# Splitting the even time steps of the filter spectra once more, by n mod 4, in a diffusion step on one Trainium2 core

## The reference, cut to what matters

```python
hdn = jnp.sin(f[0] * (z @ w1 + b1))
hdn = jnp.sin(f[1] * (hdn @ w2 + b2))
filt = (hdn @ w3).reshape(L, HYENA_ORDER, 2, B_WIDTH)
return filt * jnp.exp(-t * deltas)[:, None, None, :]
...
k = jnp.concatenate([h_fwd, jnp.zeros_like(h_fwd[:1]), jnp.flip(h_bwd[1:], axis=0)], axis=0)
y = jnp.fft.irfft(jnp.fft.rfft(u, n=2 * L, axis=1) * jnp.fft.rfft(k, axis=0)[None], n=2 * L, axis=1)[:, :L]
```

## Time and profile before

| | |
|---|---|
| time, median of 3 runs | 4553.84 us (4553.35 to 4554.28) |
| profiled execution, its time | 4552.56 us |
| its span, first to last instruction | 4550.8 us |
| mean granted TensorE clock | 0.968 |
| busy, share of the span | TensorE 94%, VectorE 28%, ScalarE 15%, GpSimd 5% |
| first tap matmul to last spectrum matmul | about 31.5 to 213.2 us |
| first load of the next stage | 222.53 us |

### The profile page before, as it was taken

The page is one execution under the profiler, slowest core; times in us unless marked ns, Lnnn a source line. Parts: engine busy times, 40 slices in busy tenths (PEclk is TensorE's granted clock), DMA queues, the critical chain, the costliest instruction groups (busy, mean ns, idle before and its releaser), DMA issues. The chain is left out here.

```text
span 4550.8 us, 61875 instructions
## 1 busy us (share of the span) xinstructions
PE 4266.9 (94%) x27077; PEld 3711.6 (82%) x27077; DVE 1258.5 (28%) x3031; ACT 678.8 (15%) x1683; POOL 239.3 (5%) x132
## 2 busy tenths in 40 slices
PE   8899988989987999999999999999978999999995
PEld 4667775577447999999998888888548999999995
DVE  5324453254372000000001453432481000000003
ACT  0022221100131101111101411111231110110111
POOL 0000000000220000000000300000220000000001
PEclk8999999999988999999999999999988999999998
DMA  7320001031325878788786301000425777777775
GB/s 278 112 84 26 26 3 30 28 138 58 105 100 185 304 290 309 287 302 298 292 293 233 114 28 44 26 24 15 153 93 204 279 271 282 276 272 280 280 276 204
DMA packets 147415, 785.41 MB, mean 173 GB/s; under 512 B 14792, under 2 KB 51304, under 8 KB 101258
## 3 DMA queue, kind: packets, MB, share of 16 engines
q1 hardware_dynamic: 137930, 747.89, 44.1%
q0 software_dynamic: 9216, 33.56, 3.5%
HBM read 725.20 MB, written 56.20 MB: 172 GB/s over the span
## 5 line engine op out<-in xcount | busy, mean ns | idle before, releaser
L1731 PE MATMUL PS<-arena 128*128 128x144 f32 x11264 | 1441.9, 287 | 8.0 <-ACT arena L1766 6.5
L1731 PEld LDWEIGHTS PS<-arena 128*128 128x128 f32 x11264 | 1406.8, 190 | 9.4 <-ACT arena L1766 7.3
L1716 PE MATMUL PS<-arena 128*128 128x144 f32 x5632 | 743.4, 286 | 0.0
L1716 PEld LDWEIGHTS PS<-arena 128*128 128x128 f32 x5632 | 711.3, 190 | 4.5 <-issue 4.5
L1824 DVE TENSOR_TENSOR arena<-PS,arena 128x144 f32<-128x144 f32 x352 | 108.4, 308 | 2006.7 <-ACT arena L1792 2006.7
L1792 ACT ACTIVATE arena<-PS 128x144 f32<-128x144 f32 x352 | 102.5, 291 | 1717.3 <-PE PS L1731 1717.3
L2204 PE MATMUL PS<-arena 128*128 128x256 f32 x1152 | 262.1, 387 | 11.0 <-DVEq L2531 11.0
L1367 PE MATMUL PS<-arena 128*128 128x512 f32 x576 | 259.4, 605 | 5.5 <-PEq L2574 5.0
L2204 PEld LDWEIGHTS PS<-arena 128*128 128x128 f32 x1152 | 221.5, 195 | 42.2 <-issue 12.1
L2156 PE MATMUL PS<-arena 128*128 128x256 f32 x1152 | 252.6, 380 | 1.7 <-ACT arena L2372 1.7
L2156 PEld LDWEIGHTS PS<-arena 128*128 128x128 f32 x1152 | 217.9, 191 | 31.7 <-issue 2.8
(11 more groups left out here) (328 smaller groups left out, 3378.0 us busy)
## 6 DMA issues: line engine op xcount, KB each, us to landing
arena<-expert_panels SPq DMA_DIRECT2D x352, 1536.0 KB
arena<-ada_w SPq DMA_DIRECT2D x6, 4096.0 KB, 14.3
arena<-ada_w SPq DMA_DIRECT2D x12, 2048.0 KB
arena<-odd_w_in SPq DMA_DIRECT2D x16, 1024.0 KB, 5.6
arena<-hgrn_w SPq DMA_DIRECT2D x20, 512.0 KB, 4.0
arena<-filter_spectra SPq DMA_DIRECT2D x36, 256.0 KB, 2.7
mid_rows<-arena SPq DMA_DIRECT2D x18, 512.0 KB, 2.9
filter_spectra<-arena SPq DMA_DIRECT2D x16, 512.0 KB, 2.7
```

Source lines behind the costliest of these rows:

```text
L1716: m = pe.matmul(PS[:, m_ // 3, m_ % 3 * SLOTS:m_ % 3 * SLOTS + SLOTS], s.w2[n % RING][:, m_ * P:(m_ + 1) * P], s.hid[:, f, :], start=f == ...
L1731: m = pe.matmul(PS[:, 6 + n % 2, q * 256:q * 256 + SLOTS], s.w13[n % RING][:, q, k, :], s.xs[e % 2][:, k, :], start=k == 0, stop=k == KD - 1)
```

## The change

The table of cosines and sines and the decay are put in another order of time steps (`by_four`): tap tiles 0 and 1 hold n mod 4 = 0, tiles 2 and 3 hold n mod 4 = 2, and 4 to 7 the odd ones as before. The tap matmuls of tiles 0 to 3 read every fourth column of `hdn` accordingly. The four steps of a round become two pairs. The first step of pair p takes the even time steps only, for frequency tile p: tiles 0 and 1 against bank 0 of the pair, tiles 2 and 3 against bank 1, 8 matmuls in all. ScalarE copies the first bank, and VectorE writes the difference (the even part of frequency tile p + 2) and the sum (the even part of tile p) to two buffers. The second step takes the odd time steps, for frequency tiles p and p + 2, 16 matmuls; VectorE reads both banks and makes sum and difference with the kept even parts, four operations, and ScalarE has nothing to do in it. Both 512 KB stores of a pair follow the second step.

```diff
@@ -61,6 +61,11 @@
         assert self.n - start == per, (self.n - start, per)
         self.base = 0
         self.n = start + count * per
+
+
+def by_four(m):
+
+    return np.concatenate([m[0::4], m[2::4], m[1::2]])
 
 
 def shape_constants():
@@ -96,9 +101,9 @@
             c["fold_fwd"] = both.reshape(2, nt, P, nt // 2, P).transpose(4, 1, 0, 3, 2).astype(np.float32)
             half = np.arange(L // 2).astype(np.float64)[None, :]
             w = np.pi * n.T * (4 * half + 1) / (2 * L)
-            w = np.concatenate([w[0::2], w[1::2]]).reshape(nt, P, nt // 2, P)
+            w = by_four(w).reshape(nt, P, nt // 2, P)
             c["spec_lat"] = (np.stack([np.cos(w), np.sin(w)]) / (2 * L)).transpose(3, 2, 0, 1, 4).astype(np.float32)
-            c["decay_lat"] = np.concatenate([dec[0::2], dec[1::2]]).reshape(nt, P, 512).transpose(1, 0, 2)
+            c["decay_lat"] = by_four(dec).reshape(nt, P, 512).transpose(1, 0, 2)
         bands = 16
         aa = np.float32(2.0 * math.pi / L) * np.arange(L, dtype=np.float32)[:, None] \
             * np.linspace(1e-4, bands - 1, bands, dtype=np.float32)[None, :]
@@ -376,6 +381,7 @@
                 s.prod = [at(x + b * 512, 2, 256) for b in range(2)]
                 s.prodc = at(x, 2, 512)
                 s.even = [at(y + b * 512, 512) for b in range(2)]
+                s.even2 = [at(z + b * 512, 512) for b in range(2)]
                 s.w1, s.w2 = at(take(64), 64, parts=33), at(take(64), 64, parts=64)
                 s.v4, s.c4 = at(take(64), 64, parts=4), at(take(4), 4, parts=64)
                 s.drow = at(take(1024), 2, 512, parts=1)
@@ -415,7 +421,9 @@
                         n += 2 if r == 0 and kt == 0 else (2 if r == 0 else 1)
                         sp.wait_ge(s.se, n)
                         i = 4 * r + kt
-                        sp.dma_start(specD[r, kt::4][0:2].rearrange("b p c n -> p b (c n)"), s.hst[i % 2]).then_inc(s.st[i % 2], 16)
+                        for t in range(2 if kt % 2 else 0):
+                            sp.dma_start(specD[r, kt // 2 + 2 * t::4][0:2].rearrange("b p c n -> p b (c n)"),
+                                         s.hst[t]).then_inc(s.st[t], 16)
                         if r == 0 and kt in (1, 3):
                             for half in range(2):
                                 sp.dma_start(specD[2 * (kt // 2) + half, 8],
@@ -431,8 +439,8 @@
                 n, o, cs = 8 * r + j, r // 2, slice(r % 2 * 256, r % 2 * 256 + 256)
                 if n >= 2:
                     pe.wait_ge(s.te, n - 1)
-                start = j % 4 * 256 + j // 4
-                pe.matmul(PS[:, n % 2, :], s.hdn[:, start:start + 255:2], s.w3[:, o, :, cs],
+                start, step = (j % 2 * 512 + j // 2 * 2, 4) if j < 4 else (j % 4 * 256 + 1, 2)
+                pe.matmul(PS[:, n % 2, :], s.hdn[:, start:start + 127 * step + 1:step], s.w3[:, o, :, cs],
                           start=True, stop=True).then_inc(s.tf, 1)
 
             def pe(s, pe):
@@ -478,16 +486,20 @@
                                 s.pe_taps(pe, r + 1, j)
                         if kt == 0:
                             pe.wait_ge(s.te, 8 * (r + 1))
+                        pair, odd = divmod(kt, 2)
                         if r == 0:
-                            pe.wait_ge(s.spl[kt], 16)
+                            pe.wait_ge(s.spl[pair], 16)
+                            if odd:
+                                pe.wait_ge(s.spl[pair + 2], 16)
                         b = 2 + n % 2 * 2
                         if n >= 2:
                             pe.wait_ge(s.se, n - 1)
-                        for par in range(2):
+                        for q in range(2):
+                            tile, j0, w = (pair + 2 * q, 4, 4) if odd else (pair, 2 * q, 2)
                             for d in range(2):
-                                for j in range(4):
-                                    mm = pe.matmul(PS[:, b + par, d * 256:d * 256 + 256], s.spec[:, kt, d, 4 * par + j, :],
-                                                   tap[:, d, 4 * par + j, :], start=j == 0, stop=j == 3)
+                                for j in range(w):
+                                    mm = pe.matmul(PS[:, b + q, d * 256:d * 256 + 256], s.spec[:, tile, d, j0 + j, :],
+                                                   tap[:, d, j0 + j, :], start=j == 0, stop=j == w - 1)
                         mm.then_inc(s.sf, 1)
                         n += 1
                         if 4 * r + kt in (1, 3, 5, 7, 9):
@@ -502,19 +514,17 @@
                 for layer in range(2):
                     act.wait_ge(s.a1, layer + 1)
                     act.activation(s.hdn, s.arg, ACT.Sin).then_inc(s.hok, 1)
-                n = 0
-                for r in range(4):
-                    for kt in range(4):
-                        if r == 0:
-                            n += 1
-                        i = 4 * r + kt
-                        act.wait_ge(s.sf, n + 1)
-                        if i >= 2:
-                            act.wait_ge(s.se, n - 1)
-                        if i == 0:
-                            act.wait_ge(s.hok, 3)
-                        act.copy(s.even[i % 2], PS[:, 2 + n % 2 * 2, :]).then_inc(s.ev, 1)
-                        n += 1
+                act.wait_ge(s.hok, 3)
+                for q in range(8):
+                    n = s.step(q // 2, q % 2 * 2)
+                    act.wait_ge(s.sf, n + 1)
+                    if q >= 2:
+                        act.wait_ge(s.se, s.step((q - 2) // 2, q % 2 * 2 + 1) + 1)
+                    act.copy(s.even[q % 2], PS[:, 2 + n % 2 * 2, :]).then_inc(s.ev, 1)
+
+            def step(s, r, kt):
+
+                return 4 * r + 4 + kt if r else 2 * kt + 1
 
             def dve_taps(s, dve, ch, r, j):
                 n, o, cs = 8 * r + j, r // 2, slice(r % 2 * 256, r % 2 * 256 + 256)
@@ -577,14 +587,22 @@
                         if r + 1 < 4:
                             for j in (2 * kt, 2 * kt + 1):
                                 s.dve_taps(dve, ch, r + 1, j)
-                        i = 4 * r + kt
+                        i, q = 4 * r + kt, 2 * r + kt // 2
+                        even = (s.even[q % 2], s.even2[q % 2])
                         dve.wait_ge(s.sf, n + 1)
-                        dve.wait_ge(s.ev, i + 1)
-                        if i >= 2:
-                            dve.wait_ge(s.st[i % 2], 16 * (i // 2))
-                        odd = PS[:, 3 + n % 2 * 2, :]
-                        dve.tensor_tensor(s.hst[i % 2][:, 0, :], s.even[i % 2], odd, ALU.add)
-                        ch.link(dve.tensor_tensor(s.hst[i % 2][:, 1, :], s.even[i % 2], odd, ALU.subtract))
+                        if kt % 2 == 0:
+                            dve.wait_ge(s.ev, q + 1)
+                            second = PS[:, 3 + n % 2 * 2, :]
+                            ch.link(dve.tensor_tensor(even[1], even[0], second, ALU.subtract))
+                            ch.link(dve.tensor_tensor(even[0], even[0], second, ALU.add))
+                        else:
+                            for t in range(2):
+                                if q:
+                                    dve.wait_ge(s.st[t], 16 * q)
+                                odd = PS[:, 2 + t + n % 2 * 2, :]
+                                dve.tensor_tensor(s.hst[t][:, 0, :], even[t], odd, ALU.add)
+                                m_ = dve.tensor_tensor(s.hst[t][:, 1, :], even[t], odd, ALU.subtract)
+                            ch.link(m_)
                         dve.engine_nop().then_inc(s.se, 1)
                         n += 1
                         if i in (1, 3, 5, 7, 9):
```

## The result

The changed kernel takes 4528.3 us (median of 6 runs, 4524.45 to 4533.75), the kernel before 4554.06 us (median of 6, 4552.94 to 4556.77). The ratio is 0.9947, 95% interval 0.9936 to 0.9958: 25.8 us less. The forecast was 4528.4. Both kernels were timed twice more later (experiment 9): over all three sets, 16 executions of the changed kernel and 23 of the kernel before, the means differ by 26.0 us (one more of the kernel before, at 10662 us, was a slow one and counts in none of these numbers).

The account below looks back on a forecast made before the run. The prediction took TensorE's matmuls to bound the filter stage: 27.6 us removed, less 0.5 for VectorE and 1.7 for stores at the end, gives 25.4 us gained and 4528.4 us. The range was 4525.2 to 4533.9 us.

Parts of the forecast that it names:

- What bounds the stage: Filter stage, about 46 to 222 us: TensorE's matmuls set the pace; ScalarE and VectorE stand idle waiting for them.
- 27.6 us of matmuls: Spectrum steps: 64 of 256 matmuls go, 8 half steps of 3.45 us, 27.6 us off TensorE.
- The first step priced like the others: First spectrum step, partly at the lower clock: its removed half lies behind the clock's rise, so also 3.45 us.
- Waits of TensorE at nothing: Spectrum PSUM banks: VectorE's added 10 us stay covered, tightest margins 0.6 to 0.7 us, so waits cost 0.
- Stores paired, never awaited: Spectrum stores leave as 8 pairs, closest 10.4 us apart, landing in 2.7 to 4.9 us and not queued behind loads.
- VectorE at the end, +0.5 us: Behind the last spectrum matmul: VectorE's four operations take 2.5 us where copy and operations took 1.96, +0.5 us.
- The last pair of stores, +1.7 us: End of the filter stage: two 512 KB stores leave together and share the DMA engines, landing 1.7 us later.
- Strided weights at nothing: Even tap matmuls reading every fourth column: weight loads cost 0 extra; upper side 1.2 us for six pairs of taps.
- The sum: 27.6 - 0.5 - 1.7 = 25.4 us gained in the filter stage, giving 4528.4 us, 0.56% less; chance 90%.
- VectorE gets late: Rival: VectorE's operations hold the spectrum banks; at worst 15.4 us gained, 4538.4 us; chance 5%.
- Slower by strided loads: Rival: even taps' weight loads outgrow their 0.43 us cover; over 9.1 us slower from 0.97 us a load; chance 2%.
- A hidden gain: Rival: a transfer sets the filter stage's end and hides the gain, 4553 us; chance 1%.

Follow-up runs that it names:

- experiment 9: Changed kernel with neighbouring tap columns, earlier first store and a half-bank signal: 4525.65 us against the changed kernel's 4526.35; timed again, 4524.59 against 4526.08.
- experiment 5: Changed kernel with the 8 matmuls of each first step issued twice: next stage's first load at 224.6 us, 27.4 behind the changed kernel.
- Experiment 6: Changed kernel with VectorE's four operations of each second step issued twice: next stage's first load at 205.3 us.
- experiment 7: Changed kernel with 4 matmuls in place of 8 in each first step: next stage's first load at 187.3 us.
- Experiment 8: Changed kernel with a separate signal so each first store leaves after two of four VectorE operations: next stage's first load at 196.4 us.
- experiments 2 to 4: Kernel before with only the new time-step order: 4558.65 us; changed kernel with neighbouring tap columns: first load 195.6 us; with every eighth column: 198.1 us.
- the repaired kernel: Changed kernel with neighbouring tap columns, earlier first store and a half-bank signal: 4525.65 us, timed again 4524.59 us.

## Why the prediction was right, point by point

- **What bounds the stage.** Right. Putting the 64 matmuls back brought 27.4 us back (experiment 5).
- **27.6 us of matmuls.** Right. A fell by 146.25 - 122.53 = 23.72 us. Seven half steps of 3.455 are 24.18, less 0.46 for four pairs of slow tap loads: 23.72.
- **The first step priced like the others.** It gained 3.55 us by the starts of the second step (66.94 and 63.39), 0.3 more than 3.45 less a pair of taps and 0.1 of a later start. The clock's rise 0.6 us earlier is worth that, and it moves from trace to trace.
- **Waits of TensorE at nothing.** Right, with the margins as reckoned (0.58 us where 0.6 was said). Experiment 6 used the margins up and TensorE waited where the prediction had put the last round's tightest place, by 1.94 us each time. The prediction went through the banks of the spectrum only; in experiment 7 TensorE waits for those of the taps and of the context spectrum as well.
- **Stores paired, never awaited.** Right; no wait of VectorE for a store shows.
- **VectorE at the end, +0.5 us.** 188.60 - 185.92 = 2.68 us against 215.35 - 213.19 = 2.16: +0.52.
- **The last pair of stores, +1.7 us.** The rest of B: 7.00 - 5.04 - 0.52 = 1.44. Experiment 8 shows that 1.33 of them come from two stores leaving together. The forecast was 0.26 too dear; its size had been worked out from loads of 4 MB.
- **Strided weights at nothing.** This step failed, and by a small sum only. The argument was that a step of two costs nothing and so four would not either. A load went from 0.19 to 0.305 us, 1.6 times. It stays under the 0.43 us of stream, and its excess shows at the head of each of the five pairs of even taps at the full clock: 0.11 x 5 = 0.6 us. The upper side had the mechanism, with six pairs and 1.2 us. The rival's count was wrong as well: there are 16 even taps and 32 such loads, not 32 and 64.
- **The sum.** 25.4 predicted for the stage, 25.3 in the pair of traces: the missed 0.6 us was made up by cheaper stores (0.26) and the earlier clock (0.3). Without what the clock gave it is 23.72 in A, 3.34 ahead of it (3.45 less one pair of taps) and 1.96 lost in B, 25.1 us. Against the one trace of the kernel before, the changed kernel's four give 24.7 to 26.3. The medians of the first set differ by 25.8. That the median came out within 0.1 us of the forecast is luck, since single runs of the changed kernel spread over 9 us.
- **The rivals.** *VectorE gets late* did not happen, but experiment 7 shows that it is the next thing to happen. *Slower by strided loads* would have needed 34.5 / 32 + 0.43 = 1.5 us a load (the prediction said 0.97, with twice the loads); even a step of eight takes 0.31. *A hidden gain* fell with experiment 5.

## What to carry to other kernels

Before matmuls are cut in a stage, reckon when the engine behind TensorE gives each bank back, place by place: here 0.6 us of margin made the whole gain real, and with four matmuls less in each first step TensorE runs into it. Then look at what the cut leaves behind the last matmul, because there every operation and every store counts in full; signals for half of a result put half of it back under the matmuls. Judge such a change by stretches of the trace that repeat to 0.02 us, when the whole time scatters by more than the terms in question.

## What the runs showed of the hardware

- A float32 weight load of 128 columns takes, at the full granted clock, 187 ns from neighbouring columns, 193 from every second, 305 from every fourth and 310 from every eighth (experiments 2 to 4). At the clock of 0.50 it takes about 0.33 us at each of these steps. Under tap matmuls with 0.43 us between loads the difference shows only behind a switch of work, 0.11 us each time.
- In four traces of the same changed kernel the granted clock fell to 0.50 between 30.8 and 33.1 us, around the first taps, and rose in the first spectrum step between 57.0 and 59.4 us; the second spectrum step then began anywhere from 62.41 to 64.02 us. In the repaired kernel's second trace the rise lay at 56.0.
- The second of two 512 KB stores was complete 1.3 us later behind its issue when the first had left 0.36 us ahead of it than when it had left 1.3 us ahead (experiment 8).
- Two idle gaps of TensorE of 1.94 us, 10.6 us apart: after the first the next 48 passes took 10.6 us, as without a gap; after the second the granted clock was 0.50 for 3.4 us, which cost 1.8. This second wait cost twice its length, 2.2 + 1.8 us.
